# Output projection begun with the recurrent half of the first token group, its operands left in the projection's memory, and the attention norm spread between its tiles

## What is computed

```python
def block_output(x, o_r, o_a, attn_out_norm, w_out, norm2, w_up, w_down):
    o_a = rms_norm(o_a, attn_out_norm)                       # attention half, 512 wide
    h = x + jnp.concatenate([o_r, o_a], axis=-1) @ w_out      # recurrent half o_r, 512 wide
    u = rms_norm(h, norm2) @ w_up
    return h + jnp.square(jax.nn.relu(u)) @ w_down            # hidden 4096
```

## Time and profile before

| | us |
|---|---|
| median of 3 runs | 1636.96 |
| profiled execution, own time | 1637.65 |
| its span in the trace | 1635.9 |
| PE busy | 1519.7 |
| DVE, ACT, POOL busy | 729.3, 589.2, 132.0 |
| heads' last PE instruction starts | 676.04 |
| first instruction of `mix_heads` | 680.49 |
| first matmul of `project_out` | 708.76 |
| first matmul of `mlp` | 840.97 |

### The profile page before, as it was taken

The page is one execution under the profiler, slowest core; times in us unless marked ns, Lnnn a source line. Parts: engine busy times, 40 slices in busy tenths (PEclk is TensorE's granted clock), DMA queues, the critical chain, the costliest instruction groups (busy, mean ns, idle before and its releaser), DMA issues. The chain is left out here.

```text
span 1635.9 us, 37435 instructions
## 1 busy us (share of the span) xinstructions
PE 1519.7 (93%) x15843; PEld 1435.8 (88%) x15843; DVE 729.3 (45%) x1211; ACT 589.2 (36%) x1225; POOL 132.0 (8%) x155
## 2 busy tenths in 40 slices
PE   6999999699989889569999999999999999999998
PEld 5999999577777777369988999999999999999998
DVE  6123333566666666351253444433344433334444
ACT  6443111466656655531134222233222223322211
POOL 3000000222222222300000000000000000000000
PEclk9999999799999999779999999999999999999999
DMA  6111110100000000141011111111011111111003
GB/s 185 44 48 39 38 51 0 33 4 4 3 4 3 4 3 5 33 129 65 26 52 52 52 52 51 28 51 51 26 51 51 38 38 51 42 35 51 26 0 110
DMA packets 81989, 66.78 MB, mean 41 GB/s; under 512 B 14385, under 2 KB 73963, under 8 KB 81867
## 3 DMA queue, kind: packets, MB, share of 16 engines
q1 hardware_dynamic: 79963, 64.42, 13.3%
q10 hardware_dynamic: 1840, 0.53, 0.1%
q0 software_dynamic: 64, 0.03, 0.0%
HBM read 59.59 MB, written 5.44 MB: 40 GB/s over the span
## 5 line engine op out<-in xcount | busy, mean ns | idle before, releaser
L102 PE MATMUL bank<-mix_hi,uw_hi 128*128 128x384 f32 (+1 forms) x768 | 252.9, 329 | 6.6 <-DVE uw_lo L1982 6.6
L102 PE MATMUL bank<-u_hi,dw_hi 128*128 128x384 f32 (+1 forms) x768 | 253.0, 329 | 5.9 <-DVE dw_lo L1987 3.6
L2002 DVE TENSOR_TENSOR hT<-hT,bank 128x384 f32<-128x384 f32 (+1 forms) x384 | 195.0, 529 | 131.3 <-PE bank L104 131.2
L104 PE MATMUL bank<-mix_hi,uw_lo 128*128 128x384 f32 (+1 forms) x768 | 252.8, 329 | 0.0
L103 PE MATMUL bank<-mix_lo,uw_hi 128*128 128x384 f32 (+1 forms) x768 | 252.7, 329 | 0.0
L103 PE MATMUL bank<-u_lo,dw_hi 128*128 128x384 f32 (+1 forms) x768 | 251.2, 327 | 0.0
L104 PE MATMUL bank<-u_hi,dw_lo 128*128 128x384 f32 (+1 forms) x768 | 251.1, 327 | 0.0
L1994 DVE TENSOR_TENSOR u_lo<-xn,u_hi 128x384 fp32r<-128x384 f32 (+1 forms) x96 | 51.5, 536 | 302.4 <-ACT u_hi L1953 302.4
L102 PE MATMUL bank<-x_hi,w_hi 128*128 128x384 f32 (+1 forms) x480 | 160.2, 334 | 0.1
L103 PE MATMUL bank<-x_lo,w_hi 128*128 128x384 f32 (+1 forms) x480 | 158.5, 330 | 0.0
L104 PE MATMUL bank<-x_hi,w_lo 128*128 128x384 f32 (+1 forms) x480 | 158.4, 330 | 0.0
(11 more groups left out here) (268 smaller groups left out, 2545.4 us busy)
## 6 DMA issues: line engine op xcount, KB each, us to landing
w_stage<-in_w_up SPq DMA_DIRECT2D x32, 512.0 KB, 4.5
d_stage<-in_w_down SPq DMA_DIRECT2D x32, 512.0 KB, 4.3
w_stage<-in_w_in SPq DMA_DIRECT2D x16, 512.0 KB, 3.8
proj<-in_x SPq DMA_DIRECT2D x9, 512.0 KB, 5.4
xs<-in_x SPq DMA_DIRECT2D x9, 512.0 KB, 5.0
w_stage<-in_w_in SPq DMA_DIRECT2D x8, 256.0 KB, 4.3
w_stage<-in_w_out SPq DMA_DIRECT2D x8, 256.0 KB, 3.1
w_stage<-in_w_out SPq DMA_DIRECT2D x16, 128.0 KB, 3.4
```

Source lines behind the costliest of these rows:

```text
L102: pe.matmul(out, hi, x_hi, start=first, stop=False)
L104: return pe.matmul(out, lo, x_hi, start=False, stop=last)
L2002: dve.tensor_tensor(hT[:, m, c:c + n], hT[:, m, c:c + n], bank[j % 6][:, 0:n], ALU.add).then_inc(dn_add.sem, 1)
```

## The change

- `mix_heads` is gone, and with it one stage and its barrier. Its work moves into `project_out`, group by group.
- The operands no longer have memory of their own. `proj` is closed ahead of the block and five tensors are laid over it tile for tile: `r_low` over tiles 0 to 3 (the lower part is written over o_r itself), `upper` over 4 to 11, `a_low` over 14 to 17 (over o_a), two spares over 12, 13 and over 18, 19. x is staged in tiles 13, 18 and 12, the first weight tile in tile 12; `d_stage` of the mlp lies in 12 and 13, `sq` and `rs` in 19. The states are stored from tile 19 instead of 9 and 10.
- The first weight tile is fetched in `phase_heads`, once the last reads of tile 12 are done.
- ACT and DVE treat four tiles of a half in one instruction, for one group. POOL makes the recurrent lower parts of groups 1 and 2.
- The squares of attention aren't added by DVE; PE takes four f32 products with ones for each group instead of one.
- PE first takes the sum of group 0, then the recurrent halves of tiles 0 to 2, then their attention halves; from tile 3 on, recurrent and attention half of each tile together. The sums of groups 1 and 2 stand behind tiles 1 and 4. Banks 6 and 7 take the sums.
- x has three slots instead of four: tiles 3 to 5 are loaded after the last tile of group 0, and 6 to 8 after that of group 1.

The diff, cut to its core (all of `mix_heads` is removed; renamings of operands are left out):

```diff
@@ phase_heads, SP
+            for name in ("zw''", "za''"):
+                sp.wait_ge(f.full_of(name), f.nth(name, LAST - 2))
+            out_fetch(sp, i, out_stage(s, 0), 0, s["wo_first"])
@@ project_out
+    xs = [proj[:, u, 0:D_MODEL] for u in (13, 18, 12)]
+    AHEAD = 3
             def _(sp):
-                for t in range(3):
-                    load_x(t)
-                for m in range(2, KT + 2):
+                out_fetch(sp, i, out_stage(s, 1), 1, wo_in[0])
+                load_x(0)
+                out_fetch(sp, i, out_stage(s, 2), 2, wo_in[1])
+                load_x(1)
+                sp.wait_ge(wo_lo_ok.sem, wo_lo_ok.n(0))
+                load_x(2)
+                for m in range(3, KT + 2):
                     sp.wait_ge(wo_hi_ok.sem, wo_hi_ok.n(m - 2))
                     sp.wait_ge(wo_lo_ok.sem, wo_lo_ok.n(m - 2))
...
                 for t in range(3, NT):
+                    sp.wait_ge(full.sem, full.n((t // 3 - 1) * KT + KT - 1))
                     load_x(t)
             def _(act):
+                recurrent(0)                 # upper part, 4 x 320
+                squares(0)
+                weights(0)
+                rstd(0)                      # waits for PE's sum: Ln, Exp
+                weights(1)
+                attention(0)                 # upper part, waits for DVE's scaled(0)
+                act.wait_ge(s["wkv_out"].sem, 32)
+                for k in range(2, NK + 2):
                     if k < KT:
+                        weights(k)
+                    if k in (2, 4):
+                        recurrent(k // 2)
+                        squares(k // 2)
+                    if k in (3, 5):
+                        rstd(k // 2)
+                    if k in (4, 6):
+                        attention(k // 2 - 1)
+                    q = k - 2
+                    act.wait_ge(read.sem, read.n(q))
+                    norm_square(act, s, v, q)
...
             def _(dve):
+                dve.wait_ge(r_hi_ok.sem, r_hi_ok.n(0))
+                dve.tensor_tensor(lower_four(0, 0), r_rows(0), upper_four(0, 0).bitcast(F32), ALU.subtract).then_inc(r_lo_ok.sem, 1)
+                weights(0)
+                scaled(0)                    # 4 scalar_tensor_tensor in place
+                weights(1)
+                attention(0)                 # lower part
+                for k in range(2, NK + 2):
                     if k < KT:
+                        weights(k)
+                    if k in (4, 6):
+                        scaled(k // 2 - 1)
+                    if k in (5, 7):
+                        attention(k // 2 - 1)
+                    q = k - 2
+                    dve.wait_ge(full.sem, full.n(q))
+                    dve.tensor_copy(hT[:, q % KT, c:c + n], bank[q % 6][:, 0:n]).then_inc(read.sem, 1)
...
+            def _(pool):
+                for g in (1, 2):
+                    pool.wait_ge(r_hi_ok.sem, r_hi_ok.n(g))
+                    pool.tensor_tensor(lower_four(0, g), r_rows(g), upper_four(0, g).bitcast(F32), ALU.subtract).then_inc(r_lo_pool.sem, 1)
             def _(pe):
+                def squared(g):
+                    pe.wait_ge(a_sq_ok.sem, a_sq_ok.n(g))
+                    for t in range(4):
+                        mm = pe.matmul(sum_bank(g), ones[:], a_squares(g)[:, t], start=t == 0, stop=t == 3)
+                    mm.then_inc(a_sum.sem, 1)
+                def recurrent(k):
...
+                    pe.wait_ge(wo_lo_ok.sem, wo_lo_ok.n(m))
+                    half(k, 0)
+                def attention(k):
...
+                    half(k, 1)               # then the residual, full, norm_sum(k - 2)
+                squared(0)
+                for k in range(AHEAD):
+                    recurrent(k)
+                for k in range(AHEAD):
+                    attention(k)
+                    if k == 1:
+                        squared(1)
+                for k in range(AHEAD, NK):
+                    recurrent(k)
+                    attention(k)
+                    if k == 4:
+                        squared(2)
```

More of the change, by code:

```diff
@@ L1284, in _ @@
             act.wait_ge(f.read_of("cen^"), f.nth("cen^", NT))
-            states = [proj[0:64, 9 + n, 0:512] for n in range(2)]
+            states = [proj[0:64, 19, 512 * n:512 * n + 512] for n in range(2)]
             for n, dst in enumerate(states):
@@ L1657, in out_fetch, with upper, lower @@
-def out_fetch(sp, i, s, m):
-    w, c, slot = i["w_out"], slice(P * m, P * m + P), m % 2
+def upper(s, t, c, n):
+    return s["parts"][1][:, t, c:c + n]
+def lower(s, t, c, n):
+    return s["parts"][0 if t < 4 else 3][:, t % 4, c:c + n]
+def out_fetch(sp, i, dst, m, done):
+    w, c = i["w_out"], slice(P * m, P * m + P)
     for rows, k, src in ((slice(0, P), slice(0, 4), w[0:512, c].rearrange("(k p) c -> p k c", p=P)),
@@ L1710, in norm_upper @@
     act.wait_ge(v["nrm_ok"].sem, v["nrm_ok"].n(k))
-    act.activation(v["x_hi"][:, k % KT, c:c + n], v["xn"][:, k % 2, 0:n], ACT.Copy).then_inc(v["nhi_ok"].sem, 1)
+    act.activation(upper(s, k % KT, c, n), v["xn"][:, k % 2, 0:n], ACT.Copy).then_inc(v["nhi_ok"].sem, 1)
 def norm_lower(dve, s, v, k):
@@ new lines, in recurrent, with squares, rstd @@
+                def recurrent(g):
+                    act.activation(upper_four(0, g), r_rows(g), ACT.Copy).then_inc(r_hi_ok.sem, 1)
+                def squares(g):
+                    act.activation(a_squares(g), a_rows(g), ACT.Square).then_inc(a_sq_ok.sem, 1)
+                def rstd(g):
+                    act.wait_ge(a_sum.sem, a_sum.n(g))
+                    act.activation(a_rstd(g), sum_bank(g), ACT.Ln, bias=eps[:, 0:1], scale=1.0 / 512).then_inc(a_ln.sem, 1)
+                    act.wait_ge(a_ln.sem, a_ln.n(g))
+                    act.activation(a_rstd(g), a_rstd(g), ACT.Exp, scale=-0.5).then_inc(a_rs_ok.sem, 1)
@@ new lines, in attention @@
+                def attention(g):
+                    act.wait_ge(a_scaled.sem, a_scaled.n(g))
+                    act.activation(upper_four(1, g), a_rows(g), ACT.Copy).then_inc(a_hi_ok.sem, 1)
+                recurrent(0)
[6 more added lines that the diff above has]
+                for k in range(2, NK + 2):
+                    if k < KT:
+                        weights(k)
[9 more added lines that the diff above has]
+                    norm_square(act, s, v, q)
+                    if q >= KT and q % KT == 2:
+                        norm_rstd(act, s, v, q // KT - 1)
+                    if q >= KT and 3 <= q % KT <= 6:
+                        for e in range(2):
+                            norm_upper(act, s, v, (q // KT - 1) * KT + 2 * (q % KT - 3) + e)
```

212 lines of the change are left out of this document (92 added, 120 removed).

## The result

| | before | changed |
|---|---|---|
| median, us | 1637.3 (4 runs, 1635.55 to 1642.9) | 1620.21 (4 runs, 1617.22 to 1622.44) |
| ratio | | 0.9886 [0.9866, 0.9905] |
| profiled execution: own time, span | 1637.65, 1635.9 | 1622.44, 1620.6 |
| heads end (first ACT instruction of the output part) | 680.49 | 678.45 |
| tile 7 full | 747.3 | 730.76 |

A second set of timings gave 0.9912 [0.989, 0.9933], 11 to 18 us. With both, I take 0.990, some 16.4 us.

What follows compares the result with a forecast made beforehand. An 18 us PE gap before the output projection, then PE ending last; tile 7 full at 683.2 + 45.8 + 6.7 = 735.7 against 747.3. 11.6 - 1.0 (clock) - 1.0 (x) = 9.6 us, so 1627.4; range 1622.5 to 1632.

Steps and rivals of the forecast that it cites:

- PE's work up to tile 7: Output projection, group 0: eight tiles with five sums 36.3 us, plus f32 sums of squares 4.3 and 5.2, together 45.8.
- When PE can start: At the join: after ACT's upper part and squares, 1.3 us each, PE starts at 683.2, 25.6 us earlier than before.
- The waits: PE in group 0: 3.1 and 1.3 us for weight tiles 1 and 2, 0.7 from POOL, 1.6 before tile 7; 6.7 together.
- the 0.7 for POOL: Group 0: POOL's lower part of group 2 stops DVE's scaling of group 1, so PE waits 0.7 us.
- The clock: After PE's early 3.1 us wait the clock may fall in the recurrent halves: 1.0 us taken, bounds 0 and 2.2.
- The x tiles: Three x slots for four: added waits at tiles 8 and 16, 1.0 us together with hand-over, bounds 0 and 5.
- Group 1 and 2 "keep their instructions": Behind tile 7: work unchanged, so everything shifts by one amount, mlp's first product near 831.4 instead of 840.97.
- A: Rival, group 0: hand-overs win, POOL stops DVE again, x and weights late; gain 2 to 6 us, about 1633; chance 0.10.
- B: Rival, output part: only the first 4.4 us of waits, full clock, x in time; gain 13.9, 1623.1 us; chance 0.07.
- C: Rival, group 0: waits keep PE's clock at half, 4.0 us more per tile; 1642.4 us with four tiles; chance 0.06.
- D: Rival, head of PE's stream: held there, recurrent half starts at 697 or so, not 687.5; about 1637 us; chance 0.05.

Runs made afterwards that it cites:

- pool_late: Changed kernel with POOL's recurrent part of group 2 made after tile 7, so it no longer meets DVE's scaling of group 1; ratio to before 0.9912.
- x_early: Changed kernel with x tiles 3 to 5 loaded into unused columns of hT before tile 7 is full; ratio to before 0.9887.
- before_moved64: Kernel before with 64 unused bytes per partition ahead of mix_hi, moving both split operands; output part 159.4 us, up projection mean 336 ns.
- before_phase: Kernel before with operands moved by 128 bytes to the weights' remainder by 256 (96); ratio to before 0.9966.
- after_phase: Changed kernel with output and mlp weights moved by 128 bytes, to remainder 224 by 256, operands at 96; ratio to before 0.9932.
- after_32: Changed kernel with everything behind last_p moved by 32 bytes per partition, operands and weights all at remainder 128; one execution, 334 to 335 ns at distance 0.
- ahead0: Changed kernel with no recurrent halves put ahead, each tile's two halves together from tile 0 on; ratio to before 0.9924.
- w0_late: Changed kernel with the first weight tile fetched at the start of project_out, not in the heads; ratio to before 0.9908.
- all_fast: Changed kernel with x tiles 3 to 5 early, weight tiles 1 and 2 split first, both norms' sums in one pass; 1608.11 us, ratio 0.9821.

## Why the prediction was wrong

The mechanism was right for the order of work, and the time was missed by a term that the prediction put at nothing: that the untouched matmuls behind tile 7 keep their speed. Point by point:

- *PE's work up to tile 7*: forecast 45.8. Measured: from 680.93 to 730.76 are 49.8, less 3.9 of waits, 45.9. Two errors cancel in it: the first sum took 0.3 less than forecast, the other two 0.14 more each (2.74 for 2.6).
- *When PE can start*: forecast 2.7 us after the join, measured 2.48.
- *The waits*: forecast 3.1 + 1.3 + 0.7 + 1.6 = 6.7, bounds 4.4 to 11. Measured 2.47 + 0.81 + 0 + 0.65 = 3.9, in the places named but one, and below the lower bound. The forecast laid full durations end to end and added hand-overs; in the rows above, ACT's second instruction starts at 679.63, where the first ends at 679.72, and the third overlaps by as much. The first sum of squares also took 3.99 and not 4.3, because the clock came up inside it. The 0.7 for POOL was a standstill that nobody waited for (pool_late).
- *The clock*: forecast 1.0 on average, measured 0 up to the mlp in both profiles of the changed kernel. It is a chance, as taken: in x_early it came up late, fell again and cost 1.2 net. The row of 838 to 841 us, from which the prediction took that a gap of 2.67 isn't followed by a fall, ends with that gap. Behind it the clock did stay up in the kernel before, but behind the same gap of 2.67 us it fell in both profiles of the changed kernel, at the start of the mlp. By the 3.4 us at half the level that is some 1.7 us, an estimate, that stands in no term. The same fall is there in 11 of the 12 profiles of the changed kernel and its variants, and in 2 of the 6 of the kernel before and its variants (before_moved64, before_phase). What brings it, no run shows.
- Together 56.2 us forecast from the join to tile 7 (2.7 + 45.8 + 6.7 + 1.0), measured 52.3.
- *The x tiles*: forecast 1.0, measured 3.2 (x_early). The three transfers asked for at tile 7 didn't bring the first or the second late, but the last: 1.4 us of wait at tile 8 and 0.75 at tile 16 alone, with short ones beside them. This is the term of the forecast's own that was most too small, by 2.2.
- *Group 1 and 2 "keep their instructions"*, and everything behind "shifted by one amount", the mlp's first product at 831.4: this is the step that failed. The instructions are the same and not their speed. Taking the operands' own memory away put them at another distance from their weights. after_phase takes that alone out of the changed kernel: 0.9932, or 11.1 us by 1637.3 (8.0 to 14.4), against the forecast's 9.6, and its 1625.57 lies in the range. Its output part, 149.4 us against 160.5, says the same 11.1; its mlp is 2.3 longer than the kernel before's, with the fall of the clock at its start. Of the roughly 16.4 us, then, some 11 are the order of work that was forecast and some 5 the placement that wasn't.

Within the 11 the errors partly cancel: 9.6 + 3.9 (up to tile 7) - 2.2 (x) = 11.3. With the 0.9 that the placement gives in the output part this is 12.2, and the marks have 12.4. That the part of the order came out near 9.6 is thus partly luck: waits put too high and x tiles put too low.

On the rivals. A did not happen: waits are fewer, though x came late, as it said. B's time of 1623.1 is near, for another reason. C, the clock in a loop, did not happen: 1.00 from 692 us to the mlp. Gaps of 2.5 and 0.8 us between bursts didn't restart it cold here, and where it did fall behind a gap in group 0 (x_early, after_32, ahead0) it was up again 3.4 to 6.8 us later. The loop that the section "HAM oscillation — how this bites in real kernels" of the Trainium skill's page TensorE: Matmul & The Clock Gate describes has waits of some 3 to 5 us, again and again; the waits here were shorter and fewer, so the prediction read more into the page than it says. D did not either: the first sum starts at 680.93. And the exclusion that the Trainium skill's page SBUF — State Buffer states in "Who interferes with whom" agrees again with the trace (5.44 us for four instructions that take 2.20 alone).

How much of the placement each stage has is less sure than its sum. In the profiles the gain of before_phase is 0.8 in the output part and 1.7 in the mlp, while the 384-column products of the up projection are busy for 3.2 us less (272.3 against 275.5). That profiled execution was the slowest of its twelve (1635.78 against a median of 1631.82), and at the start of its mlp it has the stretch of 3.4 us at the lower clock that the kernel before hasn't. This would also be why the changed kernel's mlp is only 0.7 us shorter. What the placement gives there, some 3 us (794.2 against the 797.2 of after_phase), the clock for the most part takes back: by the stretch at its start, and by one of 6.8 us from 854.8 us on, where the kernel before has one of 3.4 from 869.9.

## What to carry to other kernels

Where an edit moves buffers that matmuls read, compare the mean time of the untouched matmuls before and after: a few ns over thousands of them outweigh a saved wait, and a gap of 128 bytes gave or took 5 us here. Cut each profile at marks that every version has, and repeat the unchanged kernel, before any difference ahead of the change is explained. A standstill of an engine counts only if somebody waits for it, and of several transfers asked for at once the last was the one that PE waited for here, by more than the median said.

## What the runs showed of the hardware that was not expected

- In these runs a matmul's cadence went with how the moving operand's address stands to its weights', by remainder of 256 bytes: 0.173 us between the starts of 384-column products at distance 0 and 0.1755 at distance 128. Products of 320 columns don't follow: in the up projection, from 845 us on, 312 ns before and 311 to 312 in before_phase.
- The length of a gap alone didn't decide whether the clock fell behind it. It fell behind 1.79 (x_early), 1.83 (after_32) and 3.59 us (ahead0) and not behind 1.63 (w0_late), 1.79 (all_fast) and 2.47 (changed). Behind the 2.67 us ahead of the mlp it stayed up in both profiles of the kernel before and fell in both of the changed one.
- Stretches of some 3.4 us at the lower clock, or twice that, come and go from one execution to the next at the same places of the heads. The join moved by up to 7 us over the eighteen profiles, as much as many changes are worth.
